# Seven block products for 24 of the 32 chunks of the last feed-forward's first layer

## The chip, the cores and the metric

One core of a Trainium2 chip runs the kernel. The metric is device time in microseconds (us); the kernel before is given by the median of its runs.

## The reference

Two transformer blocks in float32 on 512 tokens of width 1024. The first has a mixer (mLSTM and sliding window attention), cross attention and a convolutional feed-forward, the second four mixers side by side and a feed-forward. The end is what the change touches:

```python
x = x + rms_norm(y, post_mix_g[l])
h = rms_norm(x, pre_mlp_g[l])
m = jnp.square(jax.nn.relu(h @ mlp_w1[l])) @ mlp_w2[l]
x = x + rms_norm(m, post_mlp_g[l])
```

`mlp_w1` is 1024x4096 (m1 in the kernel), `mlp_w2` 4096x1024 (m2).

## The kernel before

**Products.** Each float32 operand is split in two fp32r parts, hi and lo, and a product is three matmuls: hi with hi, hi with lo, lo with hi. ScalarE casts a weight chunk of 128x1024 from `stage` to `whi` (L1862), VectorE subtracts to `wlo` (L2356); activations go the same way into `xh` and `xl`.

**Weights.** SP loads chunks of 512 KB in the order of `CHUNKS` into four stage buffers (`NSTAGE`), chunk i+4 when the subtract of chunk i is done (L2993). Split chunks have six places (`NSPLIT`); chunk i frees its place when its products end (semaphore `mm`). `Plan` writes out the order by hand: each engine walks the same list of steps and performs its own, so ScalarE and VectorE are strict queues in the order of the plan. `pump` puts in as many splits as there are places. `keep` takes a place out for other data, `give` returns it.

**m1 before.** Each of 32 chunks holds all 1024 rows of 128 output features. `by_weights` (L1424 to 1426) runs 8 x 3 matmuls with the weights stationary and 512 tokens moving into one bank. ScalarE takes ReLU of the bank (L2325), VectorE multiplies it with the bank (L2957): the square stands in `hid2`.

**Seven block products.** The layers `down` (16 of 22 chunks) and m2 are already computed by a scheme for 2x2 blocks with seven products instead of eight. Tokens and rows are halved: t11, t12, t21, t22 are quarters of the activations, r1 to r4 differences of them (VectorE, L2894 to 2902); the weights are quarters or one of four sums a, b, c, d. Results are combined in PSUM with the steps `taken` (copy out of bank, L2316), `v`, `w`, `seed` (copy back, L2321), `c22`, `c21` (L2908 to 2917). There the activations are stationary and 512 weight columns move (L1628 to 1630), 12 matmuls a chunk.

**The sums.** POOL forms a to d in HBM for two groups at a time, by four plain copies (L3125) and four accumulating DMAs (L3132) of 1 MB, one at a time; each waits for the one before and for the chunk `at(n)`: every second chunk of up for n under 22, then every second from in2_c on. 48 in all. SP waits on `sums` before a stage load that reads one.

**The boundary before m1.** `boundary("out2")`: PE finishes token tile t of the layer out2, ScalarE sums squares (L2279), VectorE applies the norm and `gain` (L2932 to 2935, L2758), PE transposes the tile (L1679), ScalarE casts it (L1932), VectorE subtracts. Tile 0 instead goes through VectorE's transpose and four DMAs (`move`, L3073); ScalarE casts it in `moved` (L1937). The banks of the turns go back into a list of free banks, in order. Then three half chunks of m1 (256 tokens) are run, with turn 3 before the third, then their other halves and chunk 3 onward.

The change touches `Plan` (`out`, `turn`, `boundary`, `mlp`), the engines' steps and POOL's `at`.

## Time and profile before

| | |
|---|---|
| median of 3 runs | 1242.53 us (1241.89 to 1243.00) |
| profiled execution | 1241.57 us, of which span 1239.8 us |
| TensorE's granted clock, mean | 0.999 |
| busy: PE, VectorE, ScalarE | 1231.8, 852.6, 627.4 us |
| stage load to landing, m chunks, median | 4.2 us |
| DMA | 209.88 MB, mean 169 GB/s |

The span is the time from the first to the last instruction in the profile. PE is TensorE's matmuls, PEld its weight loads, DVE VectorE, ACT ScalarE, POOL GpSimd, SPq SP's queue. Busy time of pipelined matmuls overlaps, so distances between starts are the measure for PE.

### The profile page before, as it was taken

The page shows a single profiled execution, that of the slowest core. Times are in us where ns is not written, and L with a number is a line of the kernel's source. Part 1 is how long each engine was busy: PE and PEld are TensorE (multiplying, and loading weights), DVE is VectorE, ACT ScalarE, POOL GpSimd, SP SyncE. Part 2 cuts the span into 40 slices and gives each one's busy share as a digit, 9 for nine tenths or more (in the row PEclk, how much of TensorE's full clock was granted, in tenths as well). Part 3 has the DMA queues.
Part 4 walks back from the last instruction along what each step waited for, and adds up shares of the span by engine and source line. Part 5 has one row for each costly group of instructions (what it writes and reads, how often), then busy time and mean ns, then how long its engine had stood idle before and what let it go on. Part 6 is the DMA issues. An engine that isn't in the chain of part 4 may idle for free.

```text
span 1239.8 us, 16100 instructions
## 1 busy us (share of the span) xinstructions
PE 1231.8 (99%) x6230; PEld 1036.1 (84%) x6230; DVE 852.6 (69%) x1227; ACT 627.4 (51%) x1050; POOL 39.6 (3%) x56
## 2 busy tenths in 40 slices
PE   9999999999999999999999999999999999999998
PEld 9877898898889888888888898778898888888886
DVE  5878878576577656665688588887574444487886
ACT  5665654254446444444566464568343332355664
POOL 0000001000000000000000000000000000000000
PEclk9999999999999999999999999999999999999999
DMA  8345445422236686675775337456578676266562
GB/s 294 131 152 201 140 137 170 153 69 85 85 102 204 204 189 203 184 195 198 186 255 187 102 114 218 167 130 158 187 218 207 209 193 163 98 207 200 171 208 98
DMA packets 57925, 209.88 MB, mean 169 GB/s; under 512 B 6228, under 2 KB 13908, under 8 KB 51448
## 3 DMA queue, kind: packets, MB, share of 16 engines
q1 hardware_dynamic: 50504, 158.11, 38.8%
q0 software_dynamic: 6912, 50.33, 16.7%
q8 instruction: 50, 0.82, 0.3%
q10 hardware_dynamic: 432, 0.39, 0.1%
q14 instruction: 27, 0.22, 0.1%
HBM read 200.95 MB, written 56.10 MB: 207 GB/s over the span
## 4 chain that ended last, share of the span: by engine, by line
PE 87%; DVE 1%; ACT 1%; issue 0%; DVEq 0%
PE bank L1424 16%; PE bank L1425 16%; PE bank L1426 16%; PE bank L1630 6%; PE bank L1629 6%; PE bank L1628 6%; PE bank L1569 2%; PE bank L1573 2%; PE bank L1568 2%; PE bank L1571 2%; PE bank L1570 2%; PE bank L1572 2%; PE bank L1679 1%; PE bank L1549 1%; PE bank L1548 1%; PE bank L1547 1%
## 5 line engine op out<-in xcount | busy, mean ns | idle before, releaser
L1424 PE MATMUL bank<-xh,whi 128*128 128x512 f32 (+1 forms) x1136 | 414.2, 365 | 0.8 <-DVE R L2591 0.5
L1425 PE MATMUL bank<-xl,whi 128*128 128x512 f32 (+1 forms) x1136 | 410.4, 361 | 0.0
L1426 PE MATMUL bank<-xh,wlo 128*128 128x512 f32 (+1 forms) x1136 | 410.3, 361 | 0.0
L2356 DVE TENSOR_TENSOR wlo<-stage,whi 128x1024 fp32r<-128x1024 f32 (+1 forms) x258 | 311.2, 1212 | 105.3 <-ACT whi L1862 104.1
L1862 ACT CAST whi<-stage 128x1024 fp32r<-128x1024 f32 (+1 forms) x258 | 266.3, 1039 | 69.2 <-PE bank L1630 29.2
L1424 PEld LDWEIGHTS bank<-xh,whi 128*128 128x128 f32 x1136 | 214.5, 189 | 38.5 <-issue 5.5
L1426 PEld LDWEIGHTS bank<-xh,wlo 128*128 128x128 f32 x1136 | 214.5, 189 | 32.8
L1425 PEld LDWEIGHTS bank<-xl,whi 128*128 128x128 f32 x1136 | 214.6, 189 | 31.8 <-issue 0.2
L1629 PE MATMUL bank<-wlo,xh 128*128 128x512 f32 x328 | 127.7, 389 | 0.0
L1630 PE MATMUL bank<-whi,xl 128*128 128x512 f32 x328 | 127.7, 389 | 0.0
L1628 PE MATMUL bank<-whi,xh 128*128 128x512 f32 x328 | 127.7, 389 | 0.0
L2957 DVE TENSOR_TENSOR R<-bank,R 128x512 f32<-128x512 f32 x32 | 22.1, 692 | 82.1 <-ACT R L2325 82.1
L2325 ACT ACTIVATE R<-bank 128x512 f32<-128x512 f32 x32 | 19.1, 598 | 110.7 <-PE bank L1426 110.7
L1629 PEld LDWEIGHTS bank<-wlo,xh 128*128 128x128 f32 x328 | 61.6, 188 | 12.8
L1628 PEld LDWEIGHTS bank<-whi,xh 128*128 128x128 f32 x328 | 61.6, 188 | 12.8
L1630 PEld LDWEIGHTS bank<-whi,xl 128*128 128x128 f32 x328 | 61.6, 188 | 12.7
L2730 DVE SCALAR_TENSOR_TENSOR R<-R,par 128x512 f32<-128x512 f32 x44 | 33.1, 752 | 53.5 <-ACT R L2103 53.5
L2100 ACT COPY R<-bank 128x512 f32<-128x512 f32 x44 | 25.8, 587 | 83.4 <-PE bank L1426 83.4
L2390 DVE TENSOR_TENSOR xl<-R,xh 128x512 fp32r<-128x512 f32 x76 | 51.2, 686 | 3.6 <-ACT xh L1899 2.8
L2782 DVE SCALAR_TENSOR_TENSOR R<-R,par 128x512 f32<-128x512 f32 x60 | 41.7, 745 | 1.6 <-ACT R L2146 1.4
L1568 PE MATMUL bank<-whi,xh 128*128 128x512 f32 x102 | 40.3, 395 | 0.0
L1569 PE MATMUL bank<-whi,xh 128*128 128x512 f32 x102 | 39.8, 390 | 0.0
(387 smaller groups left out, 1577.6 us busy)
## 6 DMA issues: line engine op xcount, KB each, us to landing
stage<-in_W_m SPq DMA_DIRECT2D x56, 512.0 KB, 4.2
stage<-in_W_up SPq DMA_DIRECT2D x44, 512.0 KB, 4.1
stage<-in_W_in_a SPq DMA_DIRECT2D x19, 512.0 KB, 3.6
stage<-in_W_down SPq DMA_DIRECT2D x18, 512.0 KB, 4.1
stage<-in_W_out SPq DMA_DIRECT2D x16, 512.0 KB, 4.0
m_a<-in_W_m POOLq DMA_DIRECT2D x8, 1024.0 KB, 7.9
m_b<-in_W_m POOLq DMA_DIRECT2D x8, 1024.0 KB, 8.1
stage<-in_W_in_b SPq DMA_DIRECT2D x10, 512.0 KB, 5.1
```

Of the source, the lines that this page charges most:

```text
L1424: e.matmul(b[:, cols], hi[:, k, :], xh[:, k, cols], start=(k == 0), stop=False)
L1425: e.matmul(b[:, cols], hi[:, k, :], xl[:, k, cols], start=False, stop=False)
L1426: last = e.matmul(b[:, cols], lo[:, k, :], xh[:, k, cols], start=False, stop=(k == 7))
L1568: e.matmul(b[0][:], a_hi, hi[:, 0:512], start=(k == 0), stop=False, skip_group_check=seeded)
L1569: e.matmul(b[1][:], a_hi, hi[:, 512:1024], start=(k == 0), stop=False, skip_group_check=seeded)
L1628: e.matmul(b[:], x[:, c], hi, start=new, stop=False, skip_group_check=True)
L1629: e.matmul(b[:], x[:, c], lo, start=False, stop=False, skip_group_check=True)
L1630: last = e.matmul(b[:], z[:, c], hi, start=False, stop=end, skip_group_check=True)
L1862: e.copy(whi[:, plan.place[i], 0:width(i)], stage[:, s, 0:width(i)]).then_inc(S["w_hi"])
L2356: e.tensor_tensor(wlo[:, plan.place[i], c], stage[:, i % NSTAGE, c], whi[:, plan.place[i], c].bitcast(F32), ALU.subtract).then_inc(S["w_lo"])
L2390: e.tensor_tensor(lo, source_of(name, k), hi.bitcast(F32), ALU.subtract).then_inc(S["x_lo"])
L2782: v = e.scalar_tensor_tensor(out=cy[c], in0=cz[c][:, k:k + 512], scalar=P("cdw", 2 * k + c), in1=cy[c], op0=ALU.mult, op1=ALU.add)
```

## The change

m1's first 8 chunks (`PLAIN`) stay as they are. The other 24 become six groups of four feature tiles, each computed by seven products in the order r2, t11, r1, r3, t12, r4, t22: 42 chunks, so m1 has 50. Each holds 512 rows of 256 features; weights stay stationary and 256 tokens move (`seven_feat`). r1, r2, r3 of the activations are split once and kept in three weight places; r4 overwrites t21 in `xh`/`xl`. The differences are formed from raw x, which ScalarE copies out: `moved` gets a second copy, `keep_raw` copies the turns' banks, which are free only then. Results are combined per group, then ReLU and square by quarters. POOL forms sums for m1 too (72 operations), from the chunks of xq on. `NSPLIT` becomes 7; the buffer `more` goes. m2's first splits wait for all but m1's last chunk instead of half of it. The diff, cut:

```diff
@@ -17,7 +17,7 @@
 ALPHA = 2.0 ** 0.25
 BIG = 1e30
 CH = 1024
-NSTAGE, NSPLIT = 4, 6
+NSTAGE, NSPLIT = 4, 7
 TAIL = {"down": 6, "m2": 6}
 
 PCOLS = [("mcw", 32), ("mcb", 8), ("mng", 4), ("fcw", 132), ("fcb", 44), ("cdw", 62), ("cdb", 2),
...
-           ("out2", 8), ("m1", 32), ("m2", 56)]
+           ("out2", 8), ("m1", 50), ("m2", 56)]
 CHUNKS = [(n, c) for n, k in WEIGHTS for c in range(k)]
 CF_AHEAD = 5
...
 
-GROUPS = {"down": 4, "m2": 8}
+GROUPS = {"down": 4, "m1": 6, "m2": 8}
+PLAIN = 8
 SEVEN = {n: [(kind, g) for g in range(k) for kind in ("r1", "r2", "t11", "r3")]
          + [(kind, g) for g in range(k) for kind in (("t22", "t12", "r4") if g else ("t12", "r4", "t22"))]
-         for n, k in GROUPS.items()}
-LAST_X = {"down": ("up", 2 * NF1 - 1), "m2": ("m1", NF2 - 1)}
-HALVES = {"down": 3, "m2": 4}
+         for n, k in GROUPS.items() if n != "m1"}
+M1_KINDS = ("r2", "t11", "r1", "r3", "t12", "r4", "t22")
...
+    def out(self, key, *waits):
+        self.idle.append((self.bank[key][0], waits))
 
     def pump(self, most=NSPLIT):
...
@@ -195,7 +198,11 @@
         for g in range(2):
             self.fill(name, "turn", t, g)
             self.x_split(name, "turn", t, g)
-            self.out((name, "turn", t, g), "x_lo", self.x)
+            if name == "out2":
+                self.raw += 1
+                self.out((name, "turn", t, g), "x_lo", self.x, "raw", self.raw)
+            else:
+                self.out((name, "turn", t, g), "x_lo", self.x)
         self.turn_at[name, t] = self.turned
         self.turned += 2
         self.step("turn", name, t)
...
+            if t == 3:
+                self.step("keep_raw", 1)
         for o in range(3):
             if o == 2:
                 self.turn(name, 3)
+                self.step("keep_raw", 2)
             self.half(name, o)
+        self.step("keep_raw", 3)
         self.pump()
 
     def boundary_two(self, name, nk):
...
+    def m1_seven(self, i, kind, g):
+        if kind in ("r2", "t11", "r1", "r3"):
+            self.fill("m1", g, kind)
+        self.need()
+        self.step("seven_feat", i)
+        self.used += 1
+        if kind in ("r1", "r2", "r3") and g == NF2 // 4 - 1:
+            self.give(kind, "mm", CHUNK0["m1"] + PLAIN + i + 1)
+        if kind == "r2":
+            self.copy("m1", "taken", g)
+            self.step("m1_taken", g)
+            if g == PLAIN // 4:
+                self.step("x_sum", "r4")
+                self.x_split("m1", "r4")
+            if g == PLAIN // 4 + 1:
+                self.seven_first("m2")
+        elif kind == "t11":
+            self.combine("m1", "v", g)
+        elif kind == "r1":
+            self.combine("m1", "w", g)
+            self.out(("m1", g, "r1"), "combined", self.combined)
+            self.copy("m1", "seed", g)
+            self.step("m1_seed", g)
+        elif kind == "r3":
+            self.combine("m1", "c22", g)
+            self.combine("m1", "c21", g)
+            self.step("m1_last", g)
+        else:
+            if (kind, g) == ("t22", NF2 // 4 - 1):
+                self.seven_ahead("m2")
+            n = ("t12", "r4", "t22").index(kind)
+            self.step("m1_quarter", n, g)
+            self.out(("m1", g, ("t11", "r2", "r3")[n]), "m1_h", 4 * g + n + 2)
+            if n == 2 and g < NF2 // 4 - 1:
+                self.combine("m2", "r1", g)
+                self.combine("m2", "r3", g)
+        self.pump()
+
     def mlp(self):
-        for k in self.feat("m1", NF2):
-            if k == NF2 - 1:
-                self.seven_ahead("m2")
+        for k in self.feat("m1", PLAIN):
             self.step("m1", k)
             self.out(("m1", k), "m1_h", k + 1)
-            if k % 4 == 3 and k < NF2 - 1:
+            if k % 4 == 3:
                 self.combine("m2", "r1", k // 4)
                 self.combine("m2", "r3", k // 4)
-            if k == 8:
-                self.seven_first("m2")
-            if 12 <= k < 16:
-                self.step("rms_late", k - 12)
+            if k < 4:
+                self.combine("m1", ("r1", "r3", "r2", "r4")[k])
+            if 3 <= k < 6:
+                kind = ("r2", "r1", "r3")[k - 3]
+                self.keep(kind)
+                self.step("x_sum", kind)
+                self.x_split("m1", kind)
+            if k >= 4:
+                self.step("rms_late", k - 4)
+        for i, (kind, g) in enumerate(M1_SEVEN):
+            self.m1_seven(i, kind, g)
         self.step("rows", "pl")
         self.seven("m2")
         self.step("warm", 4)
...
+            def seven_feat(i):
+
+                kind, g = M1_SEVEN[i]
+                c = CHUNK0["m1"] + PLAIN + i
+                bank_kind = {"t12": "t11", "r4": "r2", "t22": "r3"}.get(kind, kind)
+                new = kind == bank_kind
+                b = fill("m1", g, kind) if new else bank_of("m1", g, bank_kind)
+                q.wait_ge(S["w_lo"], c + 1)
+                if kind[0] == "r":
+                    q.wait_ge(S["x_lo"], plan.x_at["m1", kind])
+                if kind == "t12":
+                    q.wait_ge(S["combined"], plan.combined_at["m1", "v", g])
+                elif kind == "r4":
+                    q.wait_ge(S["taken"], plan.copied_at["m1", "seed", g])
+                elif kind == "t22":
+                    q.wait_ge(S["combined"], plan.combined_at["m1", "c21", g])
+                hi, lo = (tiles(w[:, plan.place[c], :], 4) for w in (whi, wlo))
+                x, z = m1_x(kind, 0), m1_x(kind, 1)
+                for f in range(2):
+                    o, w = b[:, 256 * f:256 * f + 256], slice(128 * f, 128 * f + 128)
+                    for k in range(4):
+                        e.matmul(o, hi[:, k, w], x[:, k, :], start=(new and f == 0 and k == 0), stop=False, skip_group_check=True)
+                        e.matmul(o, hi[:, k, w], z[:, k, :], start=False, stop=False, skip_group_check=True)
+                        last = e.matmul(o, lo[:, k, w], x[:, k, :], start=False, stop=(k == 3), skip_group_check=True)
+                last.then_inc(S["mm"])
+
             def seven_ready(name, i):
                 q.wait_ge(S["w_lo"], CHUNK0[name] + i + 1)
...
+            def keep_raw(t):
+                for g in range(2):
+                    q.wait_ge(S["x_lo"], plan.x_at["out2", "turn", t, g])
+                    e.copy(raw[:, 4 * g:4 * g + 4, tok(t)], tiles(bank_of("out2", "turn", t, g)[:], 4)).then_inc(S["raw"])
+
             def moved(name, t):
                 q.wait_ge(*tile_ready(name, t))
                 q.wait_ge(*moved_at(name, t))
-                e.copy(xh[:, :, tok(t)].rearrange("p k (b c) -> p k b c", b=4),
-                       moved_in[name, t].rearrange("p (b k c) -> p k b c", b=4, k=8)).then_inc(S["x_hi"])
+                src = moved_in[name, t].rearrange("p (b k c) -> p k b c", b=4, k=8)
+                e.copy(xh[:, :, tok(t)].rearrange("p k (b c) -> p k b c", b=4), src).then_inc(S["x_hi"])
+                if name == "out2":
+                    e.copy(raw[:, :, tok(t)].rearrange("p k (b c) -> p k b c", b=4), src).then_inc(own.inc())
+
+            def x_sum(kind):
+                q.wait_ge(S["combined"], plan.combined_at["m1", kind, 0])
+                if kind == "r4":
+                    q.wait_ge(S["mm"], CHUNK0["m1"] + PLAIN)
+                elif plan.kept[kind][1]:
+                    q.wait_ge(S[plan.kept[kind][1][0]], plan.kept[kind][1][1])
+                e.copy(m1_x(kind, 0), raw_of(SUM_AT[kind])).then_inc(S["x_hi"])
+
+            def m1_taken(g):
+                q.wait_ge(S["mm"], CHUNK0["m1"] + PLAIN + M1_SEVEN.index(("r2", g)) + 1)
+                e.copy(vs[:, g % 2, :], bank_of("m1", g, "r2")[:]).then_inc(S["taken"])
+
+            def m1_seed(g):
+                q.wait_ge(S["combined"], plan.combined_at["m1", "w", g])
+                e.copy(bank_of("m1", g, "r2")[:], ws[:, g % 2, :]).then_inc(S["taken"])
+
+            def m1_quarter(n, g):
+                q.wait_ge(S["mm"], CHUNK0["m1"] + PLAIN + M1_SEVEN.index((("t12", "r4", "t22")[n], g)) + 1)
+                e.activation(t_of("m2", ("t11", "t12", "t21")[n], g), tiles(bank_of("m1", g, ("t11", "r2", "r3")[n])[:], 2),
+                             ACT.Relu).then_inc(S["m1_r"])
 
             def tokv_out(t):
...
+            def m1_combine(kind, g):
+
+                if kind[0] == "r":
+                    if kind == "r1":
+                        q.wait_ge(S["raw"], 6)
+                        q.wait_ge(S["m1_r"], 1)
+                    else:
+                        q.wait_ge(S["combined"], plan.combined_at["m1", {"r3": "r1", "r2": "r1", "r4": "r2"}[kind], 0])
+                    a, b = {"r1": ("t21", "t22"), "r3": ("t11", "t21"), "r2": ("t11", "t22"), "r4": ("t12", "t11")}[kind]
+                    v = e.tensor_tensor(raw_of(SUM_AT[kind]), raw_of(a), raw_of(b), ALU.subtract)
+                    v.then_inc(S["combined"])
+                    return
+                b1, b5, b7 = (bank_of("m1", g, k)[:] for k in ("t11", "r1", "r3"))
+                done = CHUNK0["m1"] + PLAIN + 1
+                v, w = vs[:, g % 2, :], ws[:, g % 2, :]
+                if kind == "v":
+                    q.wait_ge(S["mm"], done + M1_SEVEN.index(("t11", g)))
+                    q.wait_ge(S["taken"], plan.copied_at["m1", "taken", g])
+                    e.tensor_tensor(v, v, b1, ALU.subtract).then_inc(S["combined"])
+                elif kind == "w":
+                    q.wait_ge(S["mm"], done + M1_SEVEN.index(("r1", g)))
+                    q.wait_ge(S["combined"], plan.combined_at["m1", "v", g])
+                    e.tensor_tensor(w, v, b5, ALU.add).then_inc(S["combined"])
+                elif kind == "c22":
+                    q.wait_ge(S["mm"], done + M1_SEVEN.index(("r3", g)))
+                    q.wait_ge(S["combined"], plan.combined_at["m1", "w", g])
+                    e.tensor_tensor(t_of("m2", "t22", g), tiles(w, 2), tiles(b7, 2), ALU.subtract).then_inc(S["combined"])
+                else:
+                    e.tensor_tensor(b7, b7, v, ALU.subtract).then_inc(S["combined"])
+
+            def m1_last(g):
+                h = t_of("m2", "t22", g)
+                q.wait_ge(S["combined"], plan.combined_at["m1", "c22", g])
+                e.scalar_tensor_tensor(out=h, in0=h, scalar=0.0, in1=h, op0=ALU.max, op1=ALU.mult).then_inc(S["m1_h"])
+
+            def m1_quarter(n, g):
+                h = t_of("m2", ("t11", "t12", "t21")[n], g)
+                q.wait_ge(S["m1_r"], PLAIN + 3 * (g - PLAIN // 4) + n + 1)
+                e.tensor_tensor(h, tiles(bank_of("m1", g, ("t11", "r2", "r3")[n])[:], 2), h, ALU.mult).then_inc(S["m1_h"])
+
+            def x_sum(kind):
+                q.wait_ge(S["x_hi"], plan.x_at["m1", kind])
+                e.tensor_tensor(m1_x(kind, 1), raw_of(SUM_AT[kind]), m1_x(kind, 0).bitcast(F32), ALU.subtract
+                                ).then_inc(S["x_lo"])
+
             def combine(name, kind, g):
 
+                if name == "m1":
+                    m1_combine(kind, g)
+                    return
...
@@ -2981,13 +3175,16 @@
                     n, c = CHUNKS[i]
                     if i >= NSTAGE:
                         q.wait_ge(S["w_lo"], i - NSTAGE + 1)
-                    if n in SEVEN and c < len(SEVEN[n]):
-                        kind, g = TIMES[SEVEN[n][c][0]], SEVEN[n][c][1]
+                    block = chunk_of(n, c)
+                    if block:
+                        kind, g = TIMES[block[0]], block[1]
                         if (n, kind) in sums:
-                            q.wait_ge(S["sums"], 16 * (8 * (g // 2) + 5 + "abcd".index(kind) + (16 if n == "m2" else 0)))
+                            q.wait_ge(S["sums"], sum_ready(n, kind, g))
                         w = (sums[n, kind] if (n, kind) in sums else quarter(n, kind))[g]
                     elif n == "down":
                         w = d["W_down"][c - len(SEVEN[n]) + 16]
+                    elif n == "m1":
+                        w = d["W_m1"][4 * GROUPS[n] + c]
...
@@ -3113,10 +3310,14 @@
                 return w[2 * part:2 * part + 2].rearrange("g (r h) c -> (g r) (h c)", h=2)
 
             def at(n):
-                return CHUNK0["up"] + 2 * n + 1 if n < 22 else CHUNK0["in2_c"] + 2 * (n - 22) + 1
+                if n < 8:
+                    return CHUNK0["xq"] + n + 1
+                if n < 36:
+                    return CHUNK0["up"] + 3 * (n - 8) // 2 + 1
+                return CHUNK0["in2_c"] + (n - 36) + 1
 
             n = 0
-            for block in ("down", "m2"):
+            for block in GROUPS:
                 for part in range(GROUPS[block] // 2):
                     for name, w in COPIES:
                         q.wait_ge(S["mm"], at(n))
```

## Rows read from the trace of the kernel before

**Rows 1.** The page of the kernel before: busy time, slices, chain of waits.
```profile
PE 1231.8 (99%) x6230; PEld 1036.1 (84%) x6230; DVE 852.6 (69%) x1227; ACT 627.4 (51%) x1050; POOL 39.6 (3%) x56
...
PE 87%; DVE 1%; ACT 1%; issue 0%; DVEq 0%
```

**Rows 2.** The view of waits, PE alone: waited for, us in total, times, longest.
```profile
PE bank L1841 <- DVE R L2429: 1.2, 1, 1.2
```

**Rows 3.** Timeline of PE: start us, us, engine, line, operation, out<-in.
```profile
912.79 0.28 PE L1424 MATMUL bank<-xh,whi 128*128 128x256 f32 x1
...
923.94 0.40 PE L1424 MATMUL bank<-xh,whi 128*128 128x512 f32 x1
...
1081.72 0.39 PE L1628 MATMUL bank<-whi,first 128*128 128x512 f32 x1
```

**Rows 4.** Timeline of ScalarE at the boundary before m1.
```profile
896.56 1.05 ACT L1937 CAST xh<-R 128x1024 fp32r<-128x1024 f32 x1 [4.04 <-DMA R<-gb]
...
912.19 1.08 ACT L1932 CAST xh<-bank 128x512 fp32r<-128x512 f32 x2 [4.21 <-PE bank L1679]
```

**Rows 5.** Timelines of VectorE and PE at the same boundary.
```profile
899.38 0.17 DVE L2925 RECIPROCAL st<-st 128x1 f32<-128x1 f32 x1 [0.44 <-ACT st L2291]
...
902.48 1.23 DVE L2758 TENSOR_TENSOR R<-R,gb 128x1024 f32<-128x1024 f32 x1
...
910.18 1.23 DVE L2758 TENSOR_TENSOR R<-R,gb 128x1024 f32<-128x1024 f32 x1
...
904.93 1.03 PE L1679 MATMUL bank<-ident,R 128*128 128x128 f32 x8
...
911.56 1.04 PE L1679 MATMUL bank<-ident,R 128*128 128x128 f32 x8
```

**Rows 6.** Groups by line, whole span, then 580 to 730 us: busy, mean ns | idle before.
```profile
L2957 DVE TENSOR_TENSOR R<-bank,R 128x512 f32<-128x512 f32 x32 | 22.1, 692 | 82.1 <-ACT R L2325 82.1
...
L2325 ACT ACTIVATE R<-bank 128x512 f32<-128x512 f32 x32 | 19.1, 598 | 110.7 <-PE bank L1426 110.7
...
L2356 DVE TENSOR_TENSOR wlo<-stage,whi 128x1024 fp32r<-128x1024 f32 x39 | 47.7, 1223 | 14.1 <-ACT whi L1862 13.9
```

**Rows 7.** Timeline of SP's queue: the moved tile's DMAs.
```profile
892.10 2.51 SPq L3073 DMA_DIRECT2D R<-gb  x4
```

**Rows 8.** Stage loads' landing: beside copies, adds, adds at 918.6 to 960, and none.
```profile
DMA to landing us min/median/max: 3.5/3.6/6.3
...
DMA to landing us min/median/max: 3.4/4.3/5.9
...
DMA to landing us min/median/max: 4.2/6.4/9.5
...
DMA to landing us min/median/max: 3.1/3.2/3.5
```

**Rows 9.** Timeline of POOL: its DMA issues, idle before and releaser.
```profile
402.52 0.52 POOL L3125 DMA_DIRECT2D down_c<-in_W_down  x1 [8.59 <-DMA down_b<-in_W_down]
...
544.80 0.80 POOL L3132 DMA_DIRECT2D down_d<-down_c  x1 [10.59 <-DMA down_c<-down_a]
...
740.87 0.81 POOL L3132 DMA_DIRECT2D m_c<-m_a  x1 [131.31 <-PE bank L1426]
...
881.86 0.53 POOL L3125 DMA_DIRECT2D m_b<-in_W_m  x1 [5.38 <-DMA m_a<-in_W_m]
901.30 0.52 POOL L3125 DMA_DIRECT2D m_c<-in_W_m  x1 [18.92 <-PE bank L1573]
```

**Rows 10.** Windows: us, then busy (x) of PE, PEld, DVE, ACT, POOL; PEclk, DMA share, GB/s.
```profile
467.30:510.70 43.40, 43.40 (x193) 35.96 (x192) 26.62 (x33) 20.57 (x30) 2.09 (x4) 1.00 0.59 194
510.80:554.30 43.50, 43.50 (x193) 36.03 (x192) 25.52 (x31) 20.15 (x29) 3.28 (x4) 1.00 0.81 193
617.00:660.00 43.00, 43.00 (x192) 35.60 (x191) 36.72 (x45) 26.78 (x37) 0.00 (x0) 1.00 0.71 232
1046.00:1080.00 34.00, 34.00 (x152) 28.16 (x151) 13.55 (x16) 10.01 (x14) 0.00 (x0) 1.00 0.29 93
```

More of the change, by code:

```diff
@@ L77, in __init__ @@
         self.combined, self.combined_at = 0, {}
+        self.copied, self.copied_at = 0, {}
+        self.raw = 0
         self.mixer_one()
@@ L88, in fill @@
         self.bank[key] = self.idle.pop(0)
-    def out(self, key, sem, value):
-        self.idle.append((self.bank[key][0], (sem, value)))
+    def out(self, key, *waits):
+        self.idle.append((self.bank[key][0], waits))
     def pump(self, most=NSPLIT):
@@ L1061, in combine, with copy @@
         self.step("combine", name, kind, g)
+    def copy(self, *key):
+        self.copied += 1
+        self.copied_at[key] = self.copied
     def seven_x(self, name, i):
@@ L1096, in seven @@
                 self.pump()
+                for t in range(2):
+                    self.copy(name, "taken", t)
                 self.step("taken", name)
@@ L1104, in seven @@
                 ready = [i + 5, i + 6, i + 7]
+                for t in range(2):
+                    self.copy(name, "seed", t)
                 self.step("seed", name)
@@ L1397, in build_program, with m1_x, raw_of, chunk_of @@
         turned = [nc.dram_tensor(f"turned{u}", (128, 1024 if u % 4 else 512), F32, kind="Internal").ap() for u in range(8)]
+        def m1_x(kind, lo):
+            if kind in ("r1", "r2", "r3"):
+                return tiles((wlo if lo else whi)[:, plan.kept[kind][0], :], 4)
+            k, c = X_T["t21" if kind == "r4" else kind]
+            return (xl if lo else xh)[:, k, c]
+        def raw_of(which):
+            k, c = X_T[which]
+            return raw[:, k, c]
+        def chunk_of(name, c):
+            if name == "m1":
+                return (M1_SEVEN[c - PLAIN][0], M1_SEVEN[c - PLAIN][1] - PLAIN // 4) if c >= PLAIN else None
+            return SEVEN[name][c] if name in SEVEN and c < len(SEVEN[name]) else None
+        def sum_ready(name, kind, g):
+            n = 8 * (g // 2) + 5 + "abcd".index(kind)
+            for block in GROUPS:
+                if block == name:
+                    return 16 * n
+                n += 4 * GROUPS[block]
         sums = {(m, n): nc.dram_tensor(f"{m}_{n}", (k, 128, 1024), F32, kind="Internal").ap()
@@ L1414, in fill @@
                 b, left = plan.bank[key]
-                if left:
-                    q.wait_ge(S[left[0]], left[1])
+                for i in range(0, len(left or ()), 2):
+                    q.wait_ge(S[left[i]], left[i + 1])
                 return bank[b]
@@ L1884, in x_from @@
             def x_from(name, k):
-                if name in SEVEN and k < 4:
-                    q.wait_ge(S["half"], HALVES[name])
+                if name == "down" and k < 4:
+                    q.wait_ge(S["half"], 3)
+                elif name == "m2" and k < 4:
+                    q.wait_ge(S["mm"], CHUNK0[name] - 1)
                 else:
@@ L2235, in lru_a @@
             def lru_a():
[L2236 removed]
+                q.wait_ge(S["lam"], 2)
                 q.wait_ge(S["lru_c"], 2)
```

49 lines of the change are left out of this document (30 added, 19 removed).

## The prediction

> **What bounds the kernel now.** I read the page first. TensorE is busy for 99% of the span, and the chain that ended last runs through PE for 87% of it [rows 1]. Busy time of pipelined matmuls says little, so next come PE's waits: the longest is 1.2 us, once, at the start [rows 2]. No transfer, VectorE (69% busy) or ScalarE (51%) holds PE up. So the time is the number of matmuls times the distance between their starts, and the timeline gives that distance. In the last feed-forward's first layer (m1), chunk 3's first product starts at 923.94 and the second layer's (m2's) first at 1081.72: 29 chunks of 24 products with 512 moving columns take 157.78 us, 5.441 us a chunk or 0.2267 us a product [rows 3]. Just before stand four half chunks with 256 columns, from the same three lines: from 912.79 to 923.94 there are 93 starts, 0.1199 us each [rows 3]. Half the columns cost 53% of the time, not 50%: the weight load of 0.19 us stands beside each product, whatever its width.
>
> **Products (the whole gain).** Out go 24 chunks: 24 x 5.441 = 130.6 us. In come six groups of seven block products, 42 chunks of 2 x 4 x 3 = 24 products of 256 columns: 42 x 24 x 0.1199 = 120.9 us, 2.88 us a chunk. Difference: -9.7 us, all on the path that sets the end. The arithmetic saved is an eighth (16.3 us); the narrower product hands back 6.6. With a product above 130.6 / 1008 = 0.1296 us nothing would be gained. From other rows the new form could start 0.1199 to 0.120 us apart; its moving operand comes partly from weight places instead of xh, which I take at no cost (0 to 1 us).
>
> **The boundary before m1.** ScalarE copies raw x of token tile 0 straight after its cast. The cast from the same tile takes 1.05 us from 896.56 on [rows 4], so a second operation of that shape costs about 1.0. Behind it in ScalarE's queue stands the norm of tile 2, which starts without idling; VectorE waits for it (0.44 us before 899.38) and then works through to the gain of tile 3 at 910.18 plus 1.23 = 911.41, for which PE's transposes at 911.56 wait; those at 904.93 need the gain of 902.48, over at 903.71, 1.2 us earlier [rows 4, 5]. A shift of 1.0 is thus absorbed at the first turn and arrives at the second: +1.0 us (0 to 1.0). The six further raw copies (128x512, 0.60 us each by the ReLU of that shape [rows 6]) stand after each turn's casts, where ScalarE has 4.21 us idle before 912.19 [rows 4]; the last four delay weight casts by 2.4 us, but with seven places one more chunk is already split. They also hold turn banks longer: turn 3 takes the banks of turn 1, raw-copied by about 909 and needed at 911.5. Cost 0; if that cover were gone, 2.4 us.
>
> The moved tile's DMAs (issued 892.10) land just before 896.56, ScalarE idle for them for 4.04 us [rows 4, 7]. Today no copy of POOL is in flight then (issues at 881.86 and 901.30, the first landed 5 to 9 us later) [rows 9]; after the change one is (below). A later landing passes on one to one. The nearest rows are stage loads: median 3.2 us with nothing beside them, 3.6 beside copies, 4.3 and 6.4 beside adds [rows 8]. That bounds it by 0 and 3.2 us; by its pace POOL is then between its last copy and first add of a part, so I take 0.8, between 0.4 and 1.1.
>
> **POOL's sums.** 72 operations instead of 48. They run one at a time, and where POOL waited for its own DMA an operation took, issue and wait together, 9.1 us for a copy at 402.52, 5.9 at 881.86 and 11.4 for the add before 544.80 [rows 9]: copies 5.9 to 9.1, so 9.5 us in the mean with copies at 7.6. The new pace (one per 1.5 chunks of 5.44 us in up, one per chunk later) is faster than that, so POOL runs behind. In up 28 take 266 us from about 385, where its first copy starts today, to 651, into the down layer. From 740.87, where the first operation of that stage starts today, 36 take 340 us, to about 1082. m1's own sums are all there by 785. The last part of m2's is wanted by SP at chunk 24 of m2, 11 chunks ahead: about 1072 + 13 x 2.7 = 1107. So no wait on sums: 0; were POOL 25 us later, SP would stand still, with 30 us of chunks still ahead of PE.
>
> **Feeding m1's block products.** A chunk is eaten every 2.88 us instead of 5.44. Per group (20.2 us) ScalarE has seven casts of 1.05 and five operations of 0.60: 10.4 us [rows 4, 6]. VectorE has seven subtracts of 1.22 and ten operations of about 0.69 (v, w, c22, c21, the last square, three products, two block differences for m2): 15.5 us [rows 6]. That is 77% of VectorE, against 36.72 of 43 us today beside the down layer's seven products, where a chunk takes 2.7 us and PE never waits; the granted clock is 1.00 in every window read, the level of 2.4 GHz [rows 10]. v is needed two chunks after t11, the seed two chunks after w's product, c21 two after r3: 5.8 us each, against chains of at most 4. Four places stay free for weights (seven less the three kept for r1, r2, r3): chunk i's place is filled for chunk i+4, 8.6 us ahead, with 2.3 us of work. A stage load for chunk i+8 is issued once chunk i+4 is split, by my estimate 3.5 us after chunk i ends, and is needed 2.3 us before chunk i+8 starts: 7 x 2.88 - 3.5 - 2.3 = 14 us. Cost 0, but 1:1 beyond it. The x differences and their splits (4 x 3 operations) fall in the plain chunks, where VectorE is half idle; the last split waits for a whole chunk of 2.88 us instead of a half of 2.7: 0.
>
> **DMA.** A load costs 0.29 x 5.44 = 1.6 us of all 16 engines (1046 to 1080, no copies). Copies add (0.59 - 0.30) x 43.4 / 4 = 3.1 us each, adds (0.81 - 0.30) x 43.5 / 4 = 5.5 [rows 10]. In m1's block stage loads want 1.6 / 2.88 = 0.56; with a copy every 8.5 us the total is 0.93, with an add every 11 us 1.06. Four adds in a row are 44 us: short by 2.6 us of transfer, 1.7 loads or 4.8 us, inside the 14 - 4.3 = 9.7 us of lead [rows 8]. Cost 0 (0 to 16, below). Seven places instead of six: 0 (-0.3 to 0), nothing waits for a place today.
>
> **Sum.** The profiled execution took 1241.57 us (span 1239.8): 1241.6 - 9.7 + 1.0 + 0.8 = 1233.7. The median of the runs is 0.96 us above the profiled one: 1234.6 us.
>
> **Rivals.** (1) Loads are late in the add stretches. A stage buffer comes round after landing L, cast and subtract 2.3 and, my estimate, 2.2 us of queue: (L + 4.5) / 4 per chunk. L = 7.0 gives 2.88; L of 8.2 gives 3.18, which over 42 chunks is 12.6 us less 9.7 of lead, +3; L = 8.6 gives +7. For it: the 1.06, and a median of 6.4 and a maximum of 9.5 us between 918.6 and 960, where adds meet loads that at first come at the half chunks' pace of 2.9 us; against it: 4.3 beside adds in up, and the copies between the adds give the lead back [rows 8]. 1237.6 to 1242, chance 0.21.
> (2) Slower: the same ring of four buffers becomes the bound of the whole stage, since POOL, being behind, never leaves the DMA engines alone there. L = 9.5, the worst seen, gives 3.5 us a chunk: 42 x 0.62 = 26 us less 9.7: +16, 1250.6 us. It is slower than before from L = 8.7 us on (7.9 us of net gain and 9.7 of lead over 42 chunks make 3.30). Chance 0.10. The Trainium skill (DMA: Bandwidth & Descriptors, Queues, rings and completion order) says each engine round-robins between its queues a packet at a time; no row shows the turns, but by it one load passes during an add's 5.5 us and 2.4 in the other 3.9, 3.2 us a load, which the lead would still cover for four adds.
> (3) Faster: the distance follows the columns alone once the products run back to back. Then the eighth is gained whole, 16.3 us less 1.8: 1228.0. Against it stand 93 starts in a row at 0.1199 [rows 3]. Chance 0.04. The Trainium skill (TensorE: Matmul & The Clock Gate, Back-to-back issue gap) gives N / 2.4 ns plus 2.5, 109 ns for 256 columns, and 1008 x 0.1092 = 110 us, 20 us gained; it adds that in a stream the weight load sets the spacing too, and the trace's 0.1199 agrees with that half.
>
> **How the numbers follow.** The forecast with its own bounds (1232 to 1237.5: boundary from 0 to 4.5) has 0.65. 0.2% is 2.5 us, about what a measurement can tell from no change: under 1240.0 counts as faster. That holds the forecast, rival 3 and 0.12 of rival 1: 0.81. Within: 0.09, the rest of rival 1. Slower: 0.10. The range leaves out rivals 2 and 3 and a few hundredths at the forecast's edges: 1232 to 1242.
>
> **What would show it.** In the changed profile: starts 0.12 us apart through the stage and 121 us from its first product to m2's first; a second turn about 1 us late or more, with VectorE as releaser; POOL back to back from 741 to about 1080, most of its waits on its own DMAs; DVE near 77% in the stage; no PE wait on wlo. I am wrong if PE waits there on DVE's wlo with a stage landing as the cause, if landings exceed 8 us, or if the starts are closer than 0.115 us.

## The result, and the profile after

The change makes the kernel slower: 1257.16 us (median of 4 runs, 1254.22 to 1262.23) against 1242.21 us for the kernel before (4 runs, 1241.55 to 1243.00), a ratio of 1.0124 with a 95% interval of 1.0106 to 1.0142. The forecast was 1234.6 us, and 1257 lies outside its range. The profiled execution took 1259.82 us, of which the span is 1257.8: 18.0 us more than before. The four runs lie in two pairs, 1254.22 and 1254.50, and 1259.82 and 1262.23; the profile shows one of the upper pair, and the median stands between the pairs.

The page of the changed kernel: busy time, two of the lines of 40 slices, the two large DMA queues, and the chain that ended last, beside [rows 1].

```profile
PE 1233.3 (98%) x6662; PEld 1056.9 (84%) x6662; DVE 895.2 (71%) x1277; ACT 657.4 (52%) x1085; POOL 55.9 (4%) x80
...
PEclk9999999999999999999999999999987999999999
DMA  8445445447637878888576168778886997676562
...
q1 hardware_dynamic: 53096, 167.55, 40.1%
q0 software_dynamic: 10368, 75.50, 25.0%
...
PE 89%; DVE 5%; ACT 2%; DMA 2%; issue 2%; SPq 0%; DVEq 0%; ACTq 0%
```

Four readings. The chain, 87% PE and 1% DVE before, now runs through DVE, DMA and "issue" for 9% of the span. TensorE's clock, flat before, dips in slices 30 and 31, which are 912 to 975 us. POOL's queue moved 72 sums. And PE's busy time is only 1.5 us above that of before although the span grew by 18: the 9.6 us that the products save are in it, and so are the products that ran at the lower clock and count as busy, so the share of busy time hides both.

The waits of PE alone (waited for: us in total, times, longest), beside [rows 2]:

```profile
PE bank L1513 <- issue: 11.1, 4, 5.1
PE bank L1794 <- DVE R L2904: 4.6, 1, 4.6
PE bank L1829 <- DMA R<-turned: 1.6, 1, 1.6
```

**The block products do what was forecast.** Their first product and m2's first, on PE's timeline:

```profile
978.65 0.28 PE L1743 MATMUL bank<-whi 128*128 128x256 f32 x1
...
1099.60 0.40 PE L1717 MATMUL bank<-whi,first 128*128 128x512 f32 x1
```

1099.60 - 978.65 = 120.95 us for 1008 products, 0.1200 us apart, against 24 x 5.441 = 130.6 before: -9.6 us, and no wait of PE in between. All of the loss lies ahead of that. Chunk 3 of m1 starts at 934.63 where it started at 923.94 [rows 3]: +10.7. From there to the first block product it takes 44.0 us where five chunks of 5.441 make 27.2: +16.8. With -9.6 that gives +17.9 at m2's first product, the growth of the span but for 0.1.

**The five plain chunks: +16.8.** The chain of waits between 940 and 967 us (start, us, what):

```profile
940.25 5.06 issue
945.31 0.77 PE bank L1513
946.08 0.43 PE bank L1514
...
949.06 0.39 PE bank L1515
949.46 0.24 PE bank L1513
...
952.92 2.92 issue
...
963.14 2.93 issue
```

PE stands still three times, ahead of chunks 4, 5 and 6, for 10.9 us. "issue" says only that the profile ties the wait to no data that the product reads. What ended just before gives it away. ScalarE and VectorE at 940 us:

```profile
940.79 1.04 ACT L2070 CAST whi<-R 128x1024 fp32r<-128x1024 f32 x1
...
943.99 1.22 DVE L3078 TENSOR_TENSOR wlo<-R,whi 128x1024 fp32r<-128x1024 f32 x1
```

That is the split of the difference r2, over at 945.21; the next two subtracts of this line end at 955.74 and 965.97, and PE restarts at 945.31, 955.85 and 966.07. A plain chunk does not read r2. But `feat` in the plan hands every chunk `self.x`, the newest x split that the plan knows, and the change puts a split of a difference (`x_split("m1", kind)` after chunks 3, 4 and 5) ahead of chunks 4, 5 and 6. Each of these waits for one split more, and that split starts only when the ReLU of the chunk before is through ScalarE's queue. So PE, the bound, goes once around through ScalarE and VectorE per chunk.

The other 5.9 us are the clock. In the chain the products behind the first stop come 0.43 us apart until 949.06, then 0.23. The windows (us, then busy of PE, PEld, DVE, ACT, POOL; PEclk, DMA share, GB/s):

```profile
940.00:950.00 10.00, 4.94 (x14) 3.72 (x13) 4.26 (x5) 1.53 (x2) 1.58 (x2) 0.66 0.72 165
950.00:960.00 10.00, 7.08 (x24) 5.38 (x23) 2.19 (x4) 2.58 (x4) 0.81 (x1) 0.83 0.65 119
960.00:970.00 10.00, 7.07 (x24) 5.37 (x23) 2.19 (x4) 2.58 (x4) 0.80 (x1) 0.83 0.74 143
...
980.00:1080.00 100.00, 100.00 (x836) 100.00 (x835) 75.50 (x90) 50.83 (x64) 4.57 (x7) 1.00 0.82 253
```

The granted clock is 0.66 and 0.83 over the stretches with stops and 1.00 without; from 946 to 949 us, where all products are 0.43 us apart, it is 0.50, the lower level, 1.2 GHz. Nine of them take 949.46 - 945.31 = 4.15 us where nine at 0.227 take 2.04: 2.1 us here, 1.8 behind each of the other stops. The Trainium skill (TensorE: Matmul & The Clock Gate, Wait — 56ns, not 53.3ns?) gives 426.7 ns between starts of 512 columns at 1.2 GHz; the 0.43 here agrees.

**The boundary: +7.3, and +3.4 brought along.** The moved tile's DMAs on SP's queue, ScalarE's cast of them and its raw copy, and PE's second turn of a tile, all from the timeline, beside [rows 4, 5, 7]:

```profile
895.56 2.53 SPq L3270 DMA_DIRECT2D R<-gb  x4
...
904.96 1.05 ACT L2060 CAST xh<-R 128x1024 fp32r<-128x1024 f32 x1 [8.97 <-DMA R<-gb]
905.91 1.04 ACT L2062 COPY R<-R 128x1024 f32<-128x1024 f32 x1
...
913.09 1.97 PE L1794 MATMUL bank<-ident,R 128*128 128x128 f32 x8 [4.55 <-DVE R L2904]
```

The four DMAs' landing on SP's queue, 890 to 900 us, first before the change, then after:

```profile
DMA to landing us min/median/max: 2.5/2.6/2.6
```

```profile
DMA to landing us min/median/max: 7.5/7.7/8.1
```

The issue is 3.46 us later than before, like everything from 204 us on: the first 30 us took 1.3 us more, and PE waited 1.6 us at 128 us for a DMA `turned`. No profile of a variant below is this late by then. A shorter or equal wait for `turned` does come back in seven of their ten profiles (0.2 to 0.8 us, and 1.6 once), and in neither profile of a kernel without the block products in m1; the cause of it was not looked for. From the issue on the boundary is on its own: the DMAs take 7.7 us in place of 2.6, and ScalarE waits 8.97 us in place of 4.04. The second turn comes 4.8 us late beyond the 3.4, the third 7.3 (chunk 3 with it), since the 1.97 us for eight transposes (1.03 before) and the 18 products of 256 columns behind them are again those of the lower clock (0.50 from 916 to 918 us). In flight beside the DMAs is an add of POOL, which the prediction had priced at 0.4 to 1.1 us (POOL's timeline, beside [rows 9]):

```profile
884.44 0.83 POOL L3333 DMA_DIRECT2D m_b<-in_W_m  x1 [9.39 <-DMA m_a<-in_W_m]
894.65 0.81 POOL L3333 DMA_DIRECT2D m_c<-m_a  x1 [9.38 <-DMA m_b<-in_W_m]
904.22 0.81 POOL L3333 DMA_DIRECT2D m_d<-m_c  x1 [8.76 <-DMA m_c<-m_a]
...
1033.07 0.80 POOL L3333 DMA_DIRECT2D m_d<-m_c  x1 [9.46 <-DMA m_c<-m_a]
```

The add into m_c is issued 0.9 us ahead of the moved tile's first DMA, and it is an add, not the seam between copies and adds that I had placed there.

### The profile page after: what moved, and what is told of

Same layout as the page of the kernel before. It is cut to its first block, busy times and chain, and to the rows that moved or that the text cites. A ratio compares the mean times of both kernels' runs of the same rounds, so it can differ in the third digit from the quotient of the medians.

```text
span 1257.8 us, 17192 instructions
## 1 busy us (share of the span) xinstructions
PE 1233.3 (98%) x6662; PEld 1056.9 (84%) x6662; DVE 895.2 (71%) x1277; ACT 657.4 (52%) x1085; POOL 55.9 (4%) x80
## 4 chain that ended last, share of the span: by engine, by line
PE 89%; DVE 5%; ACT 2%; DMA 2%; issue 2%; SPq 0%; DVEq 0%; ACTq 0%
PE bank L1513 13%; PE bank L1514 13%; PE bank L1515 13%; PE bank L1717 6%; PE bank L1719 6%; PE bank L1718 6%; PE bank L1745 3%; PE bank L1744 3%; PE bank L1743 3%; PE bank L1657 2%; PE bank L1658 2%; PE bank L1660 2%; PE bank L1661 2%; PE bank L1659 2%; PE bank L1662 2%
## 5 line engine op out<-in xcount | busy, mean ns | idle before, releaser
L1513 PE MATMUL bank<-xh,whi 128*128 128x512 f32 (+1 forms) x944 | 342.6, 363 | 11.1 <-issue 11.1
L1514 PE MATMUL bank<-xl,whi 128*128 128x512 f32 (+1 forms) x944 | 338.8, 359 | 0.0
L1515 PE MATMUL bank<-xh,wlo 128*128 128x512 f32 (+1 forms) x944 | 338.6, 359 | 0.0
L1977 ACT CAST whi<-stage 128x1024 fp32r<-128x1024 f32 (+1 forms) x276 | 284.6, 1039 | 80.4 <-PE bank L1719 27.2
L1515 PEld LDWEIGHTS bank<-xh,wlo 128*128 128x128 f32 x944 | 180.8, 191 | 25.7
L1514 PEld LDWEIGHTS bank<-xl,whi 128*128 128x128 f32 x944 | 180.7, 191 | 25.2 <-issue 0.2
L1717 PE MATMUL bank<-whi,xh 128*128 128x512 f32 x328 | 127.6, 389 | 0.0
L2016 ACT CAST xh<-R 128x512 fp32r<-128x512 f32 x70 | 42.4, 616 | 35.5 <-DVE R L3096 20.2
L1743 PE MATMUL bank<-xh,whi 128*128 128x256 f32 x192 | 54.3, 283 | 0.0
L1744 PE MATMUL bank<-xl,whi 128*128 128x256 f32 x192 | 54.3, 283 | 0.0
L1745 PE MATMUL bank<-xh,wlo 128*128 128x256 f32 x192 | 54.3, 283 | 0.0
```

Source lines behind the costliest of these rows:

```text
L1513: e.matmul(b[:, cols], hi[:, k, :], xh[:, k, cols], start=(k == 0), stop=False)
L1514: e.matmul(b[:, cols], hi[:, k, :], xl[:, k, cols], start=False, stop=False)
L1515: last = e.matmul(b[:, cols], lo[:, k, :], xh[:, k, cols], start=False, stop=(k == 7))
L1717: e.matmul(b[:], x[:, c], hi, start=new, stop=False, skip_group_check=True)
L1743: e.matmul(o, hi[:, k, w], x[:, k, :], start=(new and f == 0 and k == 0), stop=False, skip_group_check=True)
L1744: e.matmul(o, hi[:, k, w], z[:, k, :], start=False, stop=False, skip_group_check=True)
```

## The experiments

Eleven runs of ten kernels were made in three groups, each group beside the kernel before on the same chip (1242.37, 1242.43 and 1242.58 us). The interval of each ratio is 1.1 to 2.4 us to either side, and those of neighbouring experiments often overlap, so what a single small edit does is read from the traces, and each trace shows one execution.

**1. The wait of the plain chunks.** The edit pins x for m1's plain chunks to the value that the plan has when the layer starts:

```diff
     def feat(self, name, n):
+        x = self.x if name == "m1" else None
         for j in range(n):
...
-                self.step("feat", name, j, self.x)
+                self.step("feat", name, j, x or self.x)
```

> The changed kernel, but m1's plain chunks wait for the splits of the four turned tiles alone, not for the newest x split in the plan. Theory (the wait): chunks 4, 5 and 6 stood 5.1, 2.9 and 2.9 us for the difference split planned just before them, and the clock fell at each; all of it goes, 16.4 us between chunk 3 and the first block product against before: 1257.2 - 16.4 = 1240.8 us, PE idle in that stretch 0. Rival (supply): the stop hid that weights were late too (stage landings beside POOL's copies); then PE stops on wlo instead and the time stays above 1250 us.

Measured: 1240.83 us, ratio 0.9979 (0.9968 to 0.9989), 16.3 us less than the changed kernel. The stops are gone: five plain chunks take 27.2 us, and the block products 1081.25 - 960.30 = 120.95. PE's longest wait now:

```profile
PE bank L1795 <- DVE R L2905: 6.2, 1, 6.2
```

The first block product on its timeline:

```profile
960.30 0.28 PE L1744 MATMUL bank<-whi 128*128 128x256 f32 x1
```

This alone turns "slower" into barely "faster". What is left of the forecast gain is eaten at the boundary: chunk 3 starts at 933.07, 9.1 us later than before, 6.2 of it the wait above, nearly all of the rest the lower clock. In the profile -9.6 + 9.1 = -0.5, and the spans differ by 0.4. The loss at the boundary is not the same in every execution: the eleven runs go from 1234.60 us, with a mean granted clock of 1.000, to 1242.28 us at 0.997.

**2. Seven places in the kernel before.** Does a seventh place cost something by itself, in a kernel with no other edit?

```diff
-NSTAGE, NSPLIT = 4, 6
+NSTAGE, NSPLIT = 4, 7
```

(`more` goes as in the change, with its users in the same regions.)

> The kernel before with seven places for split chunks (and the differences of down and m2 where the change has them), nothing else. Theory: the seventh place puts one more weight split of 1.2 us ahead of the attention's steps in VectorE's and SP's queues, R<-turned lands later and PE stops at the value product once, with a fall of the clock: +1.2 to +2.4 us, 1243.4 to 1244.6. Rival: the 3.4 us that the changed kernel was behind by 200 us came from the clock's warm-up at the start and chance; then 1242.2, no PE wait on R<-turned.

Measured: 1242.04 us, ratio 0.9998 (0.9990 to 1.0007). The places cost nothing that can be measured, and PE does not wait for R<-turned.

**3. POOL held while the moved tile travels,** with the edit of 1:

```diff
+            def after_move(n):
+                if n >= 53:
+                    q.wait_ge(*moved_at("out2", 0))
...
                         q.wait_ge(S["mm"], at(n))
+                        after_move(n)
```

> As x1, and POOL's operations from the 54th on wait until the moved tile of out2 has landed. Theory: adds in flight made the four DMAs R<-gb land 7.5 us after the last issue instead of about 2; without them ScalarE waits about 4 us, not 9, PE's 4.6 us stop and the cold clock behind it go: x1 less 5.5 us, 1235.3. Rival A: the DMAs are late for their own sake (SP's queue), then as x1. Rival B: holding POOL makes m2's sums late and gives it back, as x1 or worse, with SP's loads of m2's sums late.

**4. The raw copy of the moved tile late** as well: taken out of `moved`, made a step `keep_moved` behind the first `keep_raw`.

```diff
-                if name == "out2":
-                    e.copy(raw[...], src).then_inc(own.inc())
+            def keep_moved():
+                e.copy(raw[...], src).then_inc(own.inc())
...
             if t == 3:
                 self.step("keep_raw", 1)
+                self.step("keep_moved")
```

> As x2, and the raw copy of the moved tile stands behind the raw copy of turn 1 in ScalarE's queue instead of ahead of the norm of tile 2. Theory: the copy of 1.04 us shifts the norm, VectorE's chain and the fourth turn by 1.0 us: x2 less 1.0 us, 1234.3. Rival: the slack at the boundary swallows it once the DMA is in time: as x2 within 0.3 us.

Measured: 1238.12 us (0.9961, 0.9949 to 0.9974) and 1236.20 us (0.9946, 0.9934 to 0.9958). Both are above what was expected, by 2.8 and 1.9 us, and the third kernel's interval overlaps that of experiment 1; its trace shows the effect, the four DMAs landing after 2.6 us and ScalarE waiting 4.08. Each of the two profiles shows the fastest run of its kernel (1235.49 and 1234.11 us), so it holds only part of what the medians lost. In what they show, the boundary is not the reason. In the fourth kernel ScalarE's cast and all three turns stand where they stood before the change, within 0.1 us (its timeline):

```profile
896.50 1.05 ACT L2062 CAST xh<-R 128x1024 fp32r<-128x1024 f32 x1 [4.03 <-DMA R<-gb]
...
897.18 1.03 PE L1796 MATMUL bank<-ident,R 128*128 128x128 f32 x8
904.87 1.03 PE L1796 MATMUL bank<-ident,R 128*128 128x128 f32 x8
911.50 1.04 PE L1796 MATMUL bank<-ident,R 128*128 128x128 f32 x8
```

The loss is at the end of the block products and in the first of m2. The chain of waits there (start, us, what):

```profile
1054.66 1.23 DVE wlo L2506
1055.91 8.86 DMA stage<-m_a
1064.79 1.06 ACT whi L1979
1065.94 1.22 DVE wlo L2506
```

And two of PE's waits, the second at 1069.8 in m1 and the first at 1076.7, 4 us into m2:

```profile
PE bank L1719 <- DVE wlo L2506: 1.0, 1, 1.0
...
PE bank L1745 <- DVE bank L3068: 0.5, 1, 0.5
```

A stage load is 8.86 us on its way, its cast and subtract come late, PE waits. The block products take 121.6 us in place of 120.95. With nothing else in the way the supply has become the bound at this place, as in the prediction's first rival: loads between 950 and 1072 us take 7.3 us in the median and 11.2 at most, against 5.6 and 10.4 in experiment 1. There POOL's last operation is issued at 1048.92 while the stage begins at 960.30; here at 1054.45 while it begins at 951.1. The 9 us won ahead of the stage push its hungry part under POOL's adds.

**5. POOL earlier.** If so, POOL must be through sooner. First everything early: `at(n)` releases all but the first eight operations once xo's first chunk is done, with holds for both moved tiles. Then the same, but with m2's sums (n from 40 on) only from in2_c's first chunk on, so that POOL is quiet through the down layer, where seven block products already draw on the DMA engines [rows 10]:

```diff
-                if n < 36:
-                    return CHUNK0["up"] + 3 * (n - 8) // 2 + 1
-                return CHUNK0["in2_c"] + (n - 36) + 1
+                return CHUNK0["xo"] + 1 if n < 40 else CHUNK0["in2_c"] + 1
```

> As x3, but POOL's operations from the 9th on run back to back from the landing of xo's moved tile (about 367 us) without a pace, through up and down; from the 65th on they wait for out2's moved tile. Same transfers, earlier. Theory (supply): the 2.1 us that x3's profile is behind its sum (1230.1 us of span) are weights landing late (median 7.3, maximum 11.2 us) near the end of m1's block products, since POOL's operations ran until 1064; over by about 970 they leave the stage alone: landings of 4 us, no PE wait on wlo, 1236.2 - 2 to 3.5 = 1232.7 to 1234. The down layer now has them beside it: 0 to 3 us there. Rival (VectorE): at 77% it is the late one in m1's stage whatever DMA does; then the waits at 1063 to 1075 stay and the time is 1236.

> As x4, but from the 41st operation on POOL waits for in2_c, so that the second half of down is without them and they end at about 1040. Supply theory: down free of stalls, the end of m1's stage a little better than in x3: between x4 and x3, 1234 to 1236. Rival (VectorE): as x3, 1236.2.

Measured: 1236.84 us (0.9943, 0.9923 to 0.9962; single runs from 1232.52 to 1240.05), above its expectation, and 1233.16 us (0.9922, 0.9911 to 0.9934), below it. In both the block products take 120.95 us again with VectorE's work unchanged, so the rival (VectorE) falls. The first moves the trouble: PE now waits in the down layer, where loads from 616 to 710 us land in 6.7 us, not 4.2; ahead of the wait below its chain has a load of `down_d` that was 9.91 us on its way. PE's wait in this kernel:

```profile
PE bank L1719 <- DVE R L3106: 4.1, 1, 4.1
```

The landing of its stage loads from 616 to 710 us:

```profile
DMA to landing us min/median/max: 3.7/6.7/10.8
```

The same in the second kernel, from 616 to 710 and from 950 to 1072 us:

```profile
DMA to landing us min/median/max: 3.1/4.2/4.9
...
DMA to landing us min/median/max: 3.1/4.9/10.9
```

With the down layer quiet and POOL's last operation at 1022.71, PE has no wait that it did not have before, and the span is 1230.2 us: 1239.8 - 9.6. So the whole gain of the products can be had. The slowest load there still takes 10.9 us and costs nothing: a long landing does not stop PE by itself.

**6. Six places** in the kernel of experiment 4 (`NSPLIT` 6):

> As x3, with six places for split chunks. Theory: with three kept, three are left in m1's block products; a chunk must be split within two chunks, 5.8 us, for 2.3 us of work plus queue, and a stage load has 2.9 us less lead: the late landings of x3 reach PE earlier, +3 to +8 us, 1239 to 1244, with waits on wlo through the stage. Rival: places are not short, as x3 within 0.5 us (the seventh changed nothing in the kernel before, 1242.04 beside 1242.37).

Measured: 1238.24 us (0.9964, 0.9950 to 0.9978), 2.0 us above seven places, just under the range expected. The two intervals overlap and the kernels ran in different groups, so the medians alone don't show a difference. In the profiles PE's wait for wlo, both times early in m2, grows from 1.0 to 2.9 us, and the one in m1 from 0.5 to 1.1. So the seventh place is worth something like 2 us where three are held for r1, r2 and r3 and the loads are late; with six, one less is left to cover a late load.

**7. The boundary alone:** the edits of experiments 3 and 4 in the changed kernel, with the plain chunks' wait left in.

> The changed kernel with POOL held at the move and the late raw copy, but with the chunks' wait on the newest x split left in. If the two losses simply add: x3 plus 16.4 = 1252.6 us, three PE stops of 5.1, 2.9 and 2.9 us at chunks 4 to 6, and boundary transposes as in the kernel before. Rival (they overlap: the stops give the late weights time): less than x3 plus 14.

Measured: 1249.91 us (1.0060, 1.0047 to 1.0073): 13.7 us above experiment 4. The additive account misses by 2.7, the rival fits by its number. The two medians come from different groups and the gap is hardly beyond their intervals; the traces speak for the rival: between chunk 3 and the first block product the kernel takes 44.9 us in place of 27.2, 17.7 more, and yet its span is only 16.2 us longer. Its loads land as late as in experiment 4 (7.0 us in the median, 11.3 at most), but POOL's last operation is issued 32 us before m2's first product instead of 18, the block products take 120.95 us, and PE has no wait for wlo. What experiment 4 loses to late loads is not lost here. Two delays on one path are not a sum of their prices.

**8. The best kernel again, and its two parts put back.** The repeat is the second kernel of experiment 5. One variant has the raw copy back behind the cast; the other has only the wait on the newest split back:

```diff
-                self.step("feat", name, j, x or self.x)
+                self.step("feat", name, j, self.x)
```

> The same kernel as x5_pool_early_quiet_down, timed again beside its two variants. Theory: 1233.2 us again, within 0.7. Rival: that result was a lucky one, and this one lies nearer x3_raw_late, at 1234.5 to 1236.

> x5 with the raw copy of the moved tile back directly after its cast. Theory: it puts the third residual of chunk 3, and so the turned tile, about 1.0 us later (the third turn at about 912.5 in place of 911.45, with VectorE as the releaser of PE's wait): 1234.2 us. Rival: the price is the 1.9 us that lay between x2_fixed_pool_held and x3_raw_late: 1235.1. Second rival: the wait is swallowed, 1233.2.

> x5 with the plain chunks' wait on the newest split of the x differences put back, and nothing else. Theory: with transfers in order nothing overlaps with it, and the three stops of 11.1, 4 and 5.1 us return with the cold clock behind them: +16.4, 1249.6 us, PE's wait on 'issue' about as in the changed kernel, the block products starting at about 967.5 in place of 951.1. Rival: part of it lies in time that another delay would have taken, as between x3_raw_late and x7_boundary_only: +13.7, 1246.9.

| | median of 5 runs, us | ratio (95% interval) | to the repeat |
|---|---|---|---|
| repeat | 1232.89 | 0.9931 (0.9918 to 0.9943) | |
| raw copy early | 1233.63 | 0.9933 (0.9920 to 0.9945) | +0.7 |
| wait back | 1249.68 | 1.0069 (1.0055 to 1.0082) | +16.8 |

The repeat holds: 0.7% faster than before. The wait alone, with everything else in order, costs 16.8 us by the medians and 17.4 by the spans of the two profiles; the theory's 16.4 stands, its rival of 13.7 falls. The three stops are as long as in the changed kernel (5.06, 2.93 and 2.93 us), but 13 products run at the lower clock behind the first of them instead of nine, so chunk 3 to the first block product takes 17.7 us more here against 16.8 there. PE's waits name it as before:

```profile
PE bank L1514 <- issue: 11.1, 4, 5.1
```

The raw copy's 0.7 us is less than the medians can tell. The trace can: from the second turn to the third the repeat takes 6.63 us and the variant 7.47, with VectorE as releaser, as forecast. The variant's turns:

```profile
905.50 1.03 PE L1795 MATMUL bank<-ident,R 128*128 128x128 f32 x8
912.97 1.09 PE L1795 MATMUL bank<-ident,R 128*128 128x128 f32 x8 [0.47 <-DVE R L2905]
```

## Why the prediction was wrong

- **Products, -9.7:** right. 120.95 us for 1008 products, 0.1200 us apart; the saving is 9.6.
- **The differences' splits, 0:** this step failed: "The x differences and their splits (4 x 3 operations) fall in the plain chunks, where VectorE is half idle". I priced the work of these operations and looked for room beside PE. The room was there. What I did not read is the value that the plan hands to each plain chunk: the newest x split. With the three splits placed between the chunks, PE waits for each. Measured: +16.8 us by the trace, 16.3 by the medians when the wait is taken out of the changed kernel, 16.8 when it is put back into the best one; 10.9 is idle time, the rest the clock's lower level behind each stop. This alone makes the sign wrong. No rival held it: my slower case was the ring of stage buffers.
- **The moved tile's DMAs, 0.8 (0 to 3.2):** mis-sized, beyond my upper bound. I took it from the landing of stage loads, 3.6 to 6.4 us. The four moved DMAs take 7.7 us where they took 2.6, which makes 4.9 us of ScalarE's wait, 4.8 us at the second turn, and with the lower clock and the raw copy 7.3 at chunk 3; 9.1 in experiment 1, where the DMAs took 8.4. I also placed POOL at the seam between copies and adds; its add had started 0.9 us before. That the boundary's two parts are this step and the raw copy is shown: with POOL held the wait is 4.08 us again, and with the copy late too the turns are back in place.
- **Raw copy, +1.0:** right in place and releaser; 0.84 us in the trace.
- **POOL's sums, 0:** right that nothing waits for them, wrong in pace. From 744.11 to 1033.07 an operation was issued every 8.3 us, not every 9.5, so the last one came by 1033 and not near 1082.
- **Feeding, 0:** right while loads come in time. DVE is busy for 75.5% from 980 to 1080 us (77% forecast), and PE waits for it only behind late loads.
- **DMA in the stage, 0 (0 to 16), rival 1:** nothing in the changed kernel, where PE's stops let POOL be through by 1033. Once they are gone it is real: experiment 4's span of 1232.2 against 1230.2 with POOL early, 3.2 us by the medians (1236.20 to 1233.0, the mean of 1233.16 and 1232.89). The mechanism is rival 1's, landings of 7.3 in the median and 11.2 at most, and the size is its lower end. "If landings exceed 8 us" was my own sign for it, and it is a weak one: between 980 and 1100 us the changed kernel has landings up to 11.0 us and PE does not wait.
- **Seven places, 0:** right for the kernel before; in the changed one they are worth something like 2 us where loads are late, by medians whose intervals overlap.
- **The first 204 us, +3.4:** in no step. It is in one execution of the changed kernel; part of it, the wait for `turned`, is seen in more profiles of its variants, at 0.2 to 1.6 us, and its cause stays open. What share of it is in the median of the four runs is not known.

Put together from the traces: +16.8 wait, +7.3 boundary, +3.4 of this execution, -9.6 products, +0.1 tail: 18.0. By medians against 1242.2: the wait 16.3, the boundary and POOL's timing together 1240.83 - 1233.0 = 7.8, and what is then left 1233.0 - 1242.2 = -9.2. These three are steps from one kernel to the next, so they must add up to the 15.0 measured and are no test of the account; the tests are that the wait costs the same when it is put back, and that -9.2 is near the -9.6 of the traces. The split of the 7.8 into boundary and late loads depends on the order in which they are removed.

## What to carry to other kernels

When work is moved under a plan that keeps one counter ("the newest split", "the last copy"), read what every consumer in the new neighbourhood waits for, also those that do not touch the new data: a price for the moved operations says nothing about who is put behind them. The long waits with the releaser "issue" were here waits on a counter; what ended 0.1 us before them gave it away. And when a stall is removed, ask what it had been giving time to: here the background sums, which became the next bound and had to be moved before the last 3.2 us came.

## What the runs showed of the hardware

- A stop of TensorE of 2.9 us costs 1.8 us more behind it: nine products of 512 columns follow up to 0.43 us apart in place of 0.227. The 5.1 us stop costs 2.1 more in the changed kernel and 2.9 in experiments 7 and 8, with 13 slow products. At 256 columns (after the 4.55 us stop at the boundary) 18 products come 0.21 apart and the eight transposes take 1.97 us in place of 1.03, 2.5 us together.
- Four small DMAs (`R<-gb`, 128 KB each) that took 2.6 us took 7.7 beside one accumulating 1 MB DMA (8.4 in experiment 1), and 2.6 again with POOL held. The Trainium skill (DMA: Bandwidth & Descriptors, Queues, rings and completion order) says that an engine takes turns between its queues a packet at a time; no run here shows the turns. Such a wait would fit that rule if many packets stand ahead, which is argued and not shown.
- Stage loads of 512 KB, 3.2 us alone, took 7.3 us in the median and 11.2 at most beside copies and adds with a chunk every 2.88 us (experiment 4). With such loads and six places the runs also spread more: twelve from 1234.26 to 1243.78 us in experiment 6, where the seventeen runs of the kernel before beside them lie between 1241.80 and 1244.92.
